# A split float32 two-block model on one core: squares added ahead of the feed-forward, h passed on tile by tile, a weight half moved among squares, and the copy of y moved

## The chip, the cores and the metric

The kernel runs as one program on one core of a Trainium2 chip. The metric is the device time of one execution in microseconds (us), lower is better. A core has TensorE (PE, matmuls into eight PSUM banks), VectorE (DVE), ScalarE (ACT), GpSimd (POOL) and SyncE (SP, which here issues nearly all DMAs). Each engine runs its own list of instructions in order; they meet only at semaphores, and an instruction that waits holds back everything behind it on its engine.

## The reference

One batch of 256 tokens, width 1024, float32. Two blocks follow one another, each with two layers.

```
first_block, per layer: proj = x @ w_in -> three attention branches
   (8 MoBA heads, 8 MLA heads, 4 differential heads), each gated and merged,
   out projection, layer norm, a gated per-layer embedding
second_block, per layer i:
   h = rmsnorm(x, norm_mix[i]);  x = x + hybrid_mixer(h)     # gated conv, SSD, conformer conv
   h = rmsnorm(x, norm_ffn[i])
   i = 0: x = x + (silu(h @ w_gate) * (h @ w_up)) @ w_down   # dense, 2816 wide
   i = 1: x = x + mixture of 8 experts, 2 per token, 3584 wide
y = rmsnorm(x, norm_final)
rmsnorm(x, g) = x * rsqrt(mean(x*x) + eps) * g
```

## The kernel before, in words

**Layout.** The activation x lies in SBUF as `xT`: eight tiles (`DT = 8`) of 128 features by 256 tokens. A projection takes a weight unit of 1024 x 256 (1 MB), lands it in one of three slots of a ring, and multiplies it with all eight tiles.

**Split products.** float32 products are made of three passes in a faster format. Each operand is cut into a high part (a rounded copy) and a low part (the value less the high part). ACT makes the high part of a weight unit in two halves of 128x1024 (`split`, semaphore `hi_done`), POOL or DVE makes the low part of each half (`lo_done`), and PE adds up high x high, low-weight x high and high-weight x low. For 256 columns that is 48 matmuls a unit. A ring slot is free for SP's next DMA when the low parts of both halves are made (`slot_freed`). The high and low weight buffers have two slots each, so ACT may split unit q + 2 as soon as PE has used unit q. `after("mc0")` in `layer_body` is such a call: it waits for a landing, then splits the unit two places behind `mc0`, which is `az0`.

**First block.** The order of PE's work is the list `ORDER1`. Around `mc0` it is: `dv0`, `dv1`, the first half of `mc0`, step B1 (transposes of the probabilities of attention batch 1 into banks 4 to 6), step M (the second half of `mc0`), V1 (`pv`: probabilities times values into bank 7), A2 (`scores` of batch 2: twelve matmuls that need banks 4, 5 and 6 back, then four that need bank 7 back), then `mc1`, `mc2`. ACT copies the turned probabilities out (`take_turned(1)`, 3 copies, semaphore `pT_ready`, which V1 waits for), and copies bank 7 out (`take_y(1)`, semaphore `y_ready`, which the last four matmuls of A2 wait for). ACT's written order is: drain of `dv1`, `take_turned(1)`, both halves of `after("mc0")`, `take_y(1)`, `latent(0)`. Both layers of the first block run it.

**The three norms that the change touches.** (1) Ahead of mixer 0, (2) ahead of the feed-forward (`norm(1)`), (3) ahead of mixer 1. In each, ACT squares pairs of tiles of x, PE multiplies the eight tiles of squares with a matrix of 1/1024 to get the mean on all partitions, ACT takes Ln and Exp (`inv_std`), DVE makes h, eight instructions of one tile (L2362), ACT copies the high part of h in four pairs (`high_parts`, semaphore `hh_ready`), DVE makes the low part in four pairs after all of h (`low_part`, `hl_ready`). PE then starts on the first weight unit with `split_project_first`: high x high of tiles 0 to 3 for both column halves, low weights of the first column half for these tiles, the same for tiles 4 to 7, low weights of the second column half, and at the end high weights x low h. Between the mean and the first unit PE runs some matmuls on zeros (`keep_busy`).

**Around them.** In `norm(1)` PE runs the last output projections `wo0` to `wo3`; DVE adds each to x, ACT squares it. ACT makes the first half of the `gate` unit before Ln and Exp and the second half behind them; DVE makes the low part of the first half before h and of the second behind it. Ahead of mixer 1, x is updated by four additions on DVE (`add_sums`, semaphore `x_up`), ACT squares each pair, loads the table for Ln and Exp, waits for the mean, and after Exp makes the second high half of the unit `gv`, whose low half POOL makes.

Of the kernel before, what the change touches and what calls it, by code (L numbers as in the profile page):

```python
# [35 lines left out]
P = 128  # L36
# [223 lines left out]
def build_kernel(nc, a, out):  # L260

    ctx = ExitStack()
    with ctx:
# [172 lines left out]
        h_part, hh_ready, hl_ready = (signal(n, 4) for n in ("h_tiles_ready", "h_high_ready", "h_low_ready"))  # L436
# [34 lines left out]
        dt_neg, dt_w = signal("dt_neg_abs", 1), signal("dt_exp_plus_1", 1)  # L471
# [11 lines left out]
        centred = signal("ln_centred", 4)  # L483
        vlink = signal("vector_step")
# [229 lines left out]
        def _(pe):  # L714
# [19 lines left out]
            def split_project(b, slot, lo_at, x, count, settled=False):  # L734

                wh, wl = (w[:, slot, :].rearrange("p (k n) -> p k n", n=S) for w in (whi, wlo))
                for t in range(2):
# [9 lines left out]
                    ins.then_inc((used if t == 0 else count).h, 1)  # L747

# [384 lines left out]
            def wait_h(k):  # L1133

                return (lambda pair: pe.wait_ge(hh_ready.h, hh_ready.at(k, pair + 1)),
                        lambda pair: pe.wait_ge(hl_ready.h, hl_ready.at(k, pair + 1)))
# [22 lines left out]
            def mixer(m):  # L1159
# [39 lines left out]
                for name, _ in ORDER2:  # L1199
# [103 lines left out]
                    elif name == "gg":  # L1303
                        split_project_first(begin(name), *take_split(full2), *wait_h(2 * m))
                    else:
                        split_project(begin(name), *take_split(full2))

            def norm(n):
# [4 lines left out]
                for kk in range(DT):  # L1313
                    if kk % 2 == 0:
                        pe.wait_ge(nrm["sq"].h, 4 * (n - 1) + kk // 2 + 1)
                    ins = mm(views(0)[:, 0, :], ONES[D], sq[:, kk, :], kk == 0, kk == DT - 1)
# [39 lines left out]
            split_project_first(0, *take_split(ff_full), *wait_h(1))  # L1356
# [311 lines left out]
        def _(act):  # L1668
# [67 lines left out]
            def layer_body(layer):  # L1736
# [86 lines left out]
                drain(layer, "dv1", dv[:, :, S:512])  # L1823
                take_turned(1)

# [5 lines left out]
                after("mc0")  # L1831
                take_y(1)
# [176 lines left out]
            def high_parts(k):  # L2009

                for n in range(4):
                    act.wait_ge(h_part.h, h_part.at(k, n + 1))
                    copy(hh[:, 2 * n:2 * n + 2, :], h[:, 2 * n:2 * n + 2, :]).then_inc(hh_ready.h, 1)

            def mixer(m):
# [43 lines left out]
                act.wait_ge(dt_neg.h, dt_neg.at(m, 1))  # L2059
# [4 lines left out]
                act.wait_ge(dt_w.h, dt_w.at(m, 1))  # L2064
# [285 lines left out]
        def _(dve):  # L2350
# [214 lines left out]
            def low_part(k, n):  # L2565

                dve.wait_ge(hh_ready.h, hh_ready.at(k, n + 1))
# [16 lines left out]
            def mixer(m):  # L2584
# [15 lines left out]
                for t in range(DT):  # L2600
                    ins = stt(h[:, t, :], xT[:, t, :], q2[:, Q_NM + t:Q_NM + t + 1], rs2[:, 0, :],
                              ALU.mult, ALU.mult)
                    if t % 2:
                        ins.then_inc(h_part.h, 1)
# [585 lines left out]
```

## Time and profile before

| what | value |
|---|---|
| time, median of 3 runs | 2121.65 us (2121.0 to 2123.34) |
| the profiled execution: its own time | 2121.3 us |
| the profiled execution: span from first to last instruction | 2119.5 us |
| mean granted TensorE clock | 0.997 |
| busy: PE, DVE, ACT, POOL | 2096.3, 1416.4, 1295.4, 651.4 us |
| DMA, over the span | 529.06 MB, mean 250 GB/s |

The span is shorter than the execution's own time by 1.8 us, which lies outside the instructions. Times in rows are microseconds from the start of the span. `[0.84 <-ACT y L1673]` behind a row of a timeline means that the engine was idle for 0.84 us before it, until ACT's write to y released it. L720 is the one line where matmuls are issued, L1670 and L1673 those of ACT's functions and copies; their tiles tell them apart. A timeline merges like instructions in a row (x8), with the time from the first start to the last end.

### The profile page before, as it was taken

To read this page: it belongs to the slowest core of one execution; us is meant where nothing else is said; L and a number is where in the kernel's file an instruction comes from. 1 tells how busy PE (TensorE), PEld (TensorE's weight loads), DVE (VectorE), ACT (ScalarE), POOL (GpSimd) and SP (SyncE) were. 2 spreads that over 40 slices of the span, in tenths; PEclk is the share of its full clock that TensorE was granted. 3 is DMA by queue.
4 is the path that set the end of the run, shared out by engine and by line. 5 is a ranking of instruction groups with operands and counts; after the bars stand their busy time and mean duration, and the time that the engine had idled before them with its cause. 6 is when DMAs were issued, how large, how long until landed. Compare 5 with 4: busy or idle time off the path is not lost.

```text
span 2119.5 us, 33547 instructions
## 1 busy us (share of the span) xinstructions
PE 2096.3 (99%) x13311; PEld 1867.1 (88%) x13315; DVE 1416.4 (67%) x1437; ACT 1295.4 (61%) x1424; POOL 651.4 (31%) x316
## 2 busy tenths in 40 slices
PE   9999999999999999999999999999999999999998
PEld 8979999988999999999998888888888888888887
DVE  1555223346422774223777999999999999999997
ACT  4556545455544534444545777777777777777776
POOL 5717886726787204988101000000000000000000
PEclk9999999999999999999999999999999999999999
DMA  7434564625455425655447999999999999999995
GB/s 245 138 105 153 179 198 156 183 75 163 160 188 177 129 91 175 189 193 178 141 140 252 387 376 336 370 360 376 352 351 370 351 375 351 359 356 375 367 365 200
DMA packets 307633, 529.06 MB, mean 250 GB/s; under 512 B 11842, under 2 KB 152802, under 8 KB 307520
## 3 DMA queue, kind: packets, MB, share of 16 engines
q1 hardware_dynamic: 306496, 525.92, 70.9%
q8 instruction: 84, 1.38, 0.3%
q0 software_dynamic: 736, 1.00, 0.2%
q10 hardware_dynamic: 288, 0.52, 0.1%
q14 instruction: 29, 0.24, 0.0%
HBM read 525.84 MB, written 1.05 MB: 249 GB/s over the span
## 4 chain that ended last, share of the span: by engine, by line
PE 90%; POOL 3%; DVE 3%; ACT 2%; DMA 1%; issue 1%; SPq 0%; DVEq 0%; POOLq 0%
PE bank L720 88%; POOL weights_low L3092 3%; PE bank L1525 1%; DVE qb L2354 1%; DMA ring<-in_w_in_dram 1%; ACT sc L1670 1%; ACT weights_high L1673 0%; DVE sc L2362 0%; DMA ring<-in_w_ple_dram 0%; DVE h L2362 0%; PE bank L929 0%; PE bank L731 0%; DVE nmax L2389 0%; ACT expert_weights_high L1673 0%; ACT xT L1670 0%
## 5 line engine op out<-in xcount | busy, mean ns | idle before, releaser
L2354 DVE TENSOR_TENSOR expert_weights_low<-ring_experts,expert_weights_high 128x2048 fp32r<-128x2048 f32 x336 | 764.7, 2288 | 72.6 <-ACT expert_weights_high L1673 72.5
L1673 ACT ACTIVATE expert_weights_high<-ring_experts 128x2048 fp32r<-128x2048 f32 x336 | 646.4, 1924 | 166.3 <-PE bank L720 162.2
L3092 POOL TENSOR_TENSOR weights_low<-ring,weights_high 128x1024 fp32r<-128x1024 f32 x252 | 617.5, 2474 | 332.0 <-ACT weights_high L1673 218.8
L1673 ACT ACTIVATE weights_high<-ring 128x1024 fp32r<-128x1024 f32 x294 | 303.9, 1056 | 331.7 <-PE bank L720 293.0
L720 PE MATMUL bank<-x_high,weights_high 128*128 128x256 f32 x1024 | 229.8, 281 | 0.5 <-POOL weights_low L3092 0.4
L720 PE MATMUL bank<-x_high,weights_low 128*128 128x256 f32 x1024 | 226.2, 277 | 0.0
L720 PEld LDWEIGHTS bank<-x_high,weights_high 128*128 128x128 f32 x1024 | 183.6, 188 | 2.5 <-POOL weights_low L3092 0.8
L720 PEld LDWEIGHTS bank<-x_high,weights_low 128*128 128x128 f32 x1024 | 183.3, 188 | 0.5 <-issue 0.5
L720 PE MATMUL bank<-expert_weights_high,gathered_high 128*128 128x512 f32 x456 | 180.7, 396 | 0.4 <-DVE gathered_low L2362 0.4
L720 PE MATMUL bank<-expert_weights_high,gathered_low 128*128 128x512 f32 x456 | 177.8, 390 | 0.0
L720 PE MATMUL bank<-expert_weights_high,gathered_high_b 128*128 128x512 f32 x448 | 177.6, 396 | 0.0
L720 PE MATMUL bank<-expert_weights_high,gathered_low_b 128*128 128x512 f32 x448 | 174.7, 390 | 0.0
L720 PE MATMUL bank<-expert_weights_high,hidden_turned_low 128*128 128x512 f32 x440 | 171.3, 389 | 0.0
L720 PE MATMUL bank<-expert_weights_high,hidden_turned_high 128*128 128x512 f32 x440 | 171.2, 389 | 0.0
L720 PE MATMUL bank<-h_high,weights_high 128*128 128x256 f32 x704 | 164.0, 283 | 5.1 <-ACT h_high L1673 5.1
L720 PE MATMUL bank<-h_high,weights_low 128*128 128x256 f32 x704 | 161.6, 281 | 0.0
L720 PEld LDWEIGHTS bank<-h_high,weights_high 128*128 128x128 f32 x704 | 131.1, 192 | 7.7 <-ACT weights_high L1673 2.9
L720 PE MATMUL bank<-x_low,weights_high 128*128 128x256 f32 x1024 | 137.4, 277 | 0.0
L720 PEld LDWEIGHTS bank<-h_high,weights_low 128*128 128x128 f32 x704 | 130.6, 192 | 0.0
L720 PEld LDWEIGHTS bank<-x_low,weights_high 128*128 128x128 f32 x1024 | 126.3, 188 | 0.0
L720 PE MATMUL bank<-expert_weights_low,gathered_high 128*128 128x512 f32 x456 | 122.3, 390 | 0.0
L720 PE MATMUL bank<-expert_weights_low,gathered_high_b 128*128 128x512 f32 x448 | 120.0, 390 | 0.0
(338 smaller groups left out, 3724.7 us busy)
## 6 DMA issues: line engine op xcount, KB each, us to landing
ring_experts<-in_moe_w_gate_dram SPq DMA_DIRECT2D x112, 1024.0 KB, 6.0
ring_experts<-in_moe_w_up_dram SPq DMA_DIRECT2D x112, 1024.0 KB, 5.8
ring_experts<-in_moe_w_down_dram SPq DMA_DIRECT2D x112, 1024.0 KB, 5.4
ring<-in_w_in_dram SPq DMA_DIRECT2D x62, 1024.0 KB, 5.3
ring<-in_w_merge_dram SPq DMA_DIRECT2D x24, 1024.0 KB, 5.1
ring<-in_w_out_dram SPq DMA_DIRECT2D x14, 1024.0 KB, 5.1
ring<-in_ffn_w_gate_dram SPq DMA_DIRECT2D x11, 1024.0 KB, 5.4
ring<-in_ffn_w_up_dram SPq DMA_DIRECT2D x11, 1024.0 KB, 5.3
```

The lines of the kernel that those rows point to most:

```text
L720: ins = pe.matmul(dst, w, x, start=start, stop=stop, skip_group_check=share)
L1525: ins = pe.transpose(bank[2][:, c * P:(c + 1) * P], hd[:, c * P:(c + 1) * P], ident)
L1670: return nc.scalar.activation(dst, src, func, **kw)
L1673: return nc.scalar.activation(dst, src, ACT.Copy, scale=scale)
L2354: return nc.vector.tensor_tensor(dst, x, z, op)
L3092: nc.gpsimd.tensor_tensor(half_of(wlo[:, q_slot, :], t, width), half_of(ring[:, slot, :], t, width), half_of(whi[:, q_slot, :], t, width). ...
```

## The change

Five edits.

1. **h tile by tile.** DVE signals each tile of h, ACT copies it alone (8 copies of 128x256 for 4 of 128x512), and PE starts with a new function `split_project_h`: for each tile, high x high and low weights of the first column half, then high x high of the second, and low weights of the second too in the mixers (`staged=False`); in the feed-forward (`staged=True`) these last come when their low half is made. It waits at its start for the low weights that it needs.
2. **Two pairs of squares are added.** In mixer 0, after the third addition to x, DVE adds the squares of tiles 0 and 1 to those of tiles 2 and 3. `norm(1)` sums six tiles instead of eight.
3. **Mixer 1, ACT's order.** The table load goes ahead of the four squares, and the second high half of `gv` goes between the second and the third square.
4. **First block, ACT's order.** `after("mc0")` is taken apart: its first half goes ahead of `take_turned(1)`, then `take_turned(1)`, `take_y(1)`, and then its second half.
5. Two semaphores, `dt_neg` and `dt_w`, become one counted to two. No instruction is added by it.

```diff
+            def split_project_h(b, slot, lo_at, x, count, wait_high, wait_low, staged):
+                pe.wait_ge(hi_done.h, lo_at + 1)
+                pe.wait_ge(lo_done.h, lo_at + (0 if staged else 1))
+                for kk in range(DT):
+                    wait_high(kk)
+                    for t in range(2):
+                        mm(views(b)[:, t, :], wh[:, kk, t * P:(t + 1) * P], x[0][:, kk, :],
+                           kk == 0 and t == 0, False, share=True)
+                        if t == 0 or not staged:
+                            mm(views(b)[:, t, :], wl[:, kk, t * P:(t + 1) * P], x[0][:, kk, :], False, False, share=True)
+                if staged:
+                    pe.wait_ge(lo_done.h, lo_at + 1)
+                    for kk in range(DT):
+                        mm(views(b)[:, 1, :], wl[:, kk, P:2 * P], x[0][:, kk, :], False, False, share=True)
+                for kk in range(DT):
+                    if kk % 2 == 0:
+                        wait_low(kk // 2)
+                    for t in range(2):
+                        ins = mm(views(b)[:, t, :], wh[:, kk, t * P:(t + 1) * P], x[1][:, kk, :], False, ...)
...
# mixers' "gg" and the first gate unit of the feed-forward
-                        split_project_first(begin(name), *take_split(full2), *wait_h(2 * m))
+                        split_project_h(begin(name), *take_split(full2), *wait_h(2 * m), staged=False)
-            split_project_first(0, *take_split(ff_full), *wait_h(1))
+            split_project_h(0, *take_split(ff_full), *wait_h(1), staged=True)
...
# norm(n) on PE
+                first = 2 if n == 1 else 0
+                if n == 1:
+                    pe.wait_ge(sq_added.h, 1)
-                for kk in range(DT):
+                for kk in range(first, DT):
...
# first block, ACT
                 drain(layer, "dv1", dv[:, :, S:512])
+                after("mc0", (0,))
                 take_turned(1)
+                take_y(1)
+                after("mc0", (1,))
...
-                after("mc0")
-                take_y(1)
                 latent(0)
...
# high_parts, ACT
-                for n in range(4):
-                    act.wait_ge(h_part.h, h_part.at(k, n + 1))
-                    copy(hh[:, 2 * n:2 * n + 2, :], h[:, 2 * n:2 * n + 2, :]).then_inc(hh_ready.h, 1)
+                for t in range(DT):
+                    act.wait_ge(h_part.h, h_part.at(k, t + 1))
+                    copy(hh[:, t, :], h[:, t, :]).then_inc(hh_ready.h, 1)
...
# mixer 1, ACT
                 if m:
+                    act.preload_act_table_set(LOG_EXP)
                     for j in range(4):
                         act.wait_ge(x_up.h, j + 1)
                         square(j).then_inc(sq_ready.h, 1)
-                    act.preload_act_table_set(LOG_EXP)
+                        if j == 1:
+                            split2(SPLITS_M + 1, lambda t: act.wait_ge(ff_down.h, 4 * FD), halves=(1,))
                 b = G2.wait_full(act, m, "ms")
                 inv_std(rs2[:, 0, :], views(b)[:, 0, :], 0, d2a.h, drained2_at("ms")).then_inc(std_ready.h, 1)
-                if m:
-                    split2(SPLITS_M + 1, lambda t: act.wait_ge(ff_down.h, 4 * FD), halves=(1,))
                 high_parts(2 * m)
...
# mixer, DVE, after each addition of wo{j} to xT
+                    if m == 0 and j == 2:
+                        dve.wait_ge(nrm["sq"].h, 2)
+                        tt_(sq[:, 2:4, :], sq[:, 2:4, :], sq[:, 0:2, :], ALU.add).then_inc(sq_added.h, 1)
...
# low_part, DVE
-                dve.wait_ge(hh_ready.h, hh_ready.at(k, n + 1))
+                dve.wait_ge(hh_ready.h, hh_ready.at(k, 2 * n + 2))
```

## Rows read from the trace of the kernel before

**Rows 1.** The page, part 1: busy time and share of the span by engine.

```profile
PE 2096.3 (99%) x13311; PEld 1867.1 (88%) x13315; DVE 1416.4 (67%) x1437; ACT 1295.4 (61%) x1424; POOL 651.4 (31%) x316
```

**Rows 2.** The chain of waits, first block, layer 0: start, us, what.

```profile
93.75 5.21 DMA ring<-in_w_in_dram
98.99 2.00 ACT weights_high L1673 x2
101.00 0.49 ACT y L1673
...
101.53 13.60 PE bank L720 x84
```

**Rows 3.** ACT's timeline, the same stretch: start, us, instruction, [idle before].

```profile
94.99 1.58 ACT L1673 ACTIVATE pT<-bank 128x512 f32<-128x512 f32 x3 [1.50 <-PE bank L929]
```

**Rows 4.** PE's timeline, the same stretch.

```profile
97.62 1.57 PE L720 MATMUL bank<-pT,av 128*64 128x256 f32 x16
99.12 1.57 PE L720 MATMUL bank<-dqk 64*128 64x256 f32 x12
101.53 0.71 PE L720 MATMUL bank<-dqk 64*128 64x128 f32 x4 [0.84 <-ACT y L1673]
```

**Rows 5.** ACT's timeline, first block, layer 1.

```profile
436.74 2.00 ACT L1673 ACTIVATE weights_high<-ring 128x1024 fp32r<-128x1024 f32 x2 [2.51 <-DMA ring<-in_w_in_dram]
```

**Rows 6.** ACT's timeline ahead of mixer 0.

```profile
687.81 3.31 ACT L1670 ACTIVATE sq<-qb,par 128x256 f32<-128x256 f32 x8 [0.55 <-DVE qb L2362]
...
694.45 0.63 ACT L1673 ACTIVATE h_high<-h 128x512 fp32r<-128x512 f32 x1 [1.00 <-DVE h L2362]
```

**Rows 7.** DVE's timeline ahead of mixer 0.

```profile
693.54 3.26 DVE L2362 SCALAR_TENSOR_TENSOR h<-xT,q,rs 128x256 f32<-128x256 f32 x8 [1.05 <-issue]
696.72 2.49 DVE L2354 TENSOR_TENSOR h_low<-h,h_high 128x512 fp32r<-128x512 f32 x4
```

**Rows 8.** PE's timeline at the start of mixer 0.

```profile
695.23 1.44 PE L720 MATMUL bank<-h_high,weights_high 128*128 128x256 f32 x8 [1.01 <-ACT h_high L1673]
...
699.45 1.98 PE L720 MATMUL bank<-h_low,weights_high 128*128 128x256 f32 x16
701.26 0.28 PE L720 MATMUL bank<-h_high,weights_high 128*128 128x256 f32 x1
```

**Rows 9.** PE's timeline ahead of the feed-forward and in its first unit.

```profile
810.43 3.62 PE L720 MATMUL bank<-sq,ones 128*128 128x256 f32 x16
...
822.76 1.07 PE L720 MATMUL bank<-h_high,weights_high 128*128 128x256 f32 x8
```

**Rows 10.** DVE's timeline ahead of the feed-forward.

```profile
813.03 1.23 DVE L2354 TENSOR_TENSOR weights_low<-ring,weights_high 128x1024 fp32r<-128x1024 f32 x1 [1.71 <-ACT weights_high L1673]
815.04 3.26 DVE L2362 SCALAR_TENSOR_TENSOR h<-xT,q,rs 128x256 f32<-128x256 f32 x8 [0.78 <-ACT rs L1670]
```

**Rows 11.** ACT's timeline ahead of the feed-forward.

```profile
814.91 1.04 ACT L1673 ACTIVATE weights_high<-ring 128x1024 fp32r<-128x1024 f32 x1
```

**Rows 12.** ACT's timeline ahead of mixer 1.

```profile
995.31 1.06 ACT L1673 ACTIVATE weights_high<-ring 128x1024 fp32r<-128x1024 f32 x1 [1.66 <-PE bank L720]
...
999.40 1.28 ACT L2024 ACT_TABLE_LOAD   x1
```

**Rows 13.** DVE's timeline ahead of mixer 1.

```profile
1002.52 5.35 DVE L2362 SCALAR_TENSOR_TENSOR h<-xT,q,rs 128x256 f32<-128x256 f32 x8 [3.41 <-ACT rs L1670]
```

**Rows 14.** POOL's timeline, the same stretch.

```profile
1003.43 2.57 POOL L3092 TENSOR_TENSOR weights_low<-ring,weights_high 128x1024 fp32r<-128x1024 f32 x1 [4.58 <-ACT weights_high L1673]
```

**Rows 15.** PE's timeline ahead of mixer 1 and in its first unit.

```profile
997.83 3.61 PE L720 MATMUL bank<-sq,ones 128*128 128x256 f32 x16
...
1007.00 0.84 PE L720 MATMUL bank<-h_high,weights_high 128*128 128x256 f32 x4 [2.09 <-ACT h_high L1673]
...
1013.74 0.28 PE L720 MATMUL bank<-h_high,weights_high 128*128 128x256 f32 x1
```

**Rows 16.** Busy time by stretch: start:end, us, PE, PEld, DVE, ACT, POOL, clock, DMA share, GB/s.

```profile
1007.00:1011.00 4.00, 4.00 (x21) 4.00 (x22) 3.28 (x7) 1.26 (x2) 0.54 (x1) 0.57 0.16 12
```

More of the change, by code:

```diff
@@ L435, in build_kernel @@
         wo3_in, router_in = signal("last_out_weights_landed", 16), sem("router_weights_landed")
-        h_part, hh_ready, hl_ready = (signal(n, 4) for n in ("h_tiles_ready", "h_high_ready", "h_low_ready"))
+        h_part, hh_ready, hl_ready = (signal(n, k) for n, k in (
+            ("h_tiles_ready", DT), ("h_high_ready", DT), ("h_low_ready", 4)))
         first_units = N_UNITS1 * LAYERS
@@ L483, in build_kernel @@
         centred = signal("ln_centred", 4)
+        sq_added = signal("first_pairs_of_squares_added")
         vlink = signal("vector_step")
@@ L747, in split_project @@
                     ins.then_inc((used if t == 0 else count).h, 1)
+            def split_project_h(b, slot, lo_at, x, count, wait_high, wait_low, staged):
+                wh, wl = (w[:, slot, :].rearrange("p (k n) -> p k n", n=S) for w in (whi, wlo))
+                pe.wait_ge(hi_done.h, lo_at + 1)
[15 more added lines that the diff above has]
+                    for t in range(2):
+                        ins = mm(views(b)[:, t, :], wh[:, kk, t * P:(t + 1) * P], x[1][:, kk, :], False,
+                                 kk == DT - 1, share=True)
+                        if kk == DT - 1:
+                            ins.then_inc((used if t == 0 else count).h, 1)
             def split_project_low_last(b, slot, lo_at, x, count, halves=(0, 1)):
@@ L1312, in norm @@
                     G2.wait_drained(pe, n - 1, [g for g in G2.names if G2.index(g) % BANKS2 == 0][-1])
-                for kk in range(DT):
+                first = 2 if n == 1 else 0
+                if n == 1:
+                    pe.wait_ge(sq_added.h, 1)
+                for kk in range(first, DT):
                     if kk % 2 == 0:
                         pe.wait_ge(nrm["sq"].h, 4 * (n - 1) + kk // 2 + 1)
-                    ins = mm(views(0)[:, 0, :], ONES[D], sq[:, kk, :], kk == 0, kk == DT - 1)
+                    ins = mm(views(0)[:, 0, :], ONES[D], sq[:, kk, :], kk == first, kk == DT - 1)
                 ins.then_inc(nrm["full"].h, 1)
@@ L2063, in mixer @@
                 pad(2)
-                act.wait_ge(dt_w.h, dt_w.at(m, 1))
+                act.wait_ge(dt_step.h, dt_step.at(m, 2))
                 fn(dtt[:, 4, :], dtt[:, 3, :], ACT.Ln).then_inc(dtl.h, 1)
@@ L2715, in mixer @@
                 conv_x(2)
-                dve.wait_ge(dt_w.h, dt_w.at(m, 1))
+                dve.wait_ge(dt_step.h, dt_step.at(m, 2))
                 step_sizes()
@@ L2799, in norm @@
                     ins = stt(dst[:, t, :], xT[:, t, :], q2[:, w + t:w + t + 1], rs2[:, 0, :], ALU.mult, ALU.mult)
-                    if n == 1 and t % 2:
+                    if n == 1:
                         ins.then_inc(h_part.h, 1)
```

15 lines of the change are left out of this document (7 added, 8 removed).

## The prediction

> **What bounds the kernel now.** I read the busy times by engine first: PE is busy for 99% of the span [rows 1], and the chain of waits is nearly all PE. So a gain or a loss counts only where PE stands still, or where it is set back by something ahead of it. Then I read the chain and the timelines at the places that the diff touches.
>
> In the first block the chain at `mc0` is DMA, ACT, PE: the weights of `az0` land at 98.96 us, ACT splits both halves (2.00 us), copies y, and PE goes on at 101.53 us [rows 2]. ACT had copied the turned probabilities before that, at 94.99 us [rows 3], so that PE could run V1 at 97.62 us, right behind the second half of `mc0`, and stood idle only 0.84 us ahead of the last four matmuls of A2 [rows 4]. Layer 1 has the same wait of ACT for the landing [rows 5]. At the three norms PE waits for std, h and h's high parts [rows 8, 9 and 15].
>
> **Edit 4, ACT's order at mc0.** The reader should see that the half now put ahead of `take_turned(1)` can't start before its weights land, and that nothing in the change makes them land sooner: the transfer is issued at 93.75 us and takes 5.21 us, behind POOL's low parts [rows 2]. So ACT, which took up the probabilities at 94.99 us, now stands at the wait until 98.99 us. Queued behind it are the probabilities, y and the second half, and PE waits for the first of them. One half takes 1.00 us (two took 2.00), so `take_turned(1)` runs from 99.99 to 101.57 us (1.58 us) [rows 3], and V1 starts near 101.6 us instead of 97.62 us: PE is idle for 4.0 us in one piece. V1 and the first twelve matmuls of A2 take 3.07 us (97.62 us to where the idle 0.84 us began, 100.69 us) [rows 4]. y is copied during those twelve matmuls, so the old wait of 0.84 us goes. The last four matmuls start near 101.6 + 3.07 = 104.65 us instead of 101.53 us: 3.1 us later. PE is the chain for the 13.60 us behind this point [rows 2], and the softmax of batch 2 starts from those same scores, so I see no cover that takes it back. The second half of `az0` is done near 104.7 us, long before its use behind `mc2`, `uq` and the rest. Two layers: **+6.2 us**.
>
> **The clock in these stalls.** Ahead of mixer 1 PE stood still for most of 1003 to 1007 us (one idle piece of 2.09 us at its end) [rows 15], and behind it the granted clock was 0.57 over 4 us [rows 16], which is a time mostly at the lower level, 1.2 GHz. That costs (1 - 0.57) x 4 = 1.7 us of PE's work. A stall of 4.0 us in one piece is longer than that one. Bounds for each layer: 0, if the clock stays up, and 2 x 1.7 = 3.4 us, if two such stretches follow. I take 1.4 us, near the row, and less than it because part of the slow stretch can fall into the idle time itself. Two layers: **+2.8 us**.
>
> The Trainium skill, "TensorE: Matmul & The Clock Gate", section "Why this matters for your kernels", says that idle gaps between bursts of matmuls bring the engine back to its half rate. By that rule both stalls are followed by a slow stretch, which is what the row ahead of mixer 1 shows; without it the sum below would be 2.8 us less.
>
> **Edit 1 ahead of mixer 0.** DVE makes the eight tiles in 3.26 us, 0.40 us apart (the last takes 0.48) [rows 7]. ACT's first copy started 0.91 us behind DVE's start, after two tiles, and PE 0.78 us behind that [rows 6 and 8]. With one tile: the tile is there at 0.50 us, ACT's copy of 256 columns takes 0.49 us (eight squares of that size took 3.31 us, so they follow each other 0.40 us apart, even with a wait each) [rows 6], and PE needs 0.15 us more: start near 693.54 + 1.16 = 694.7 us instead of 695.23 us. PE then has four matmuls a tile. Sixteen take 1.81 us (699.45 to 701.26 us) [rows 8], so four take 0.45 us, longer than ACT's 0.40 us: PE is not starved. 32 matmuls end at 694.7 + 3.63 = 698.3 us, and the sixteen with low h at 700.15 us. The low parts come 0.62 us apart from 696.72 us on, the last at 699.2 us [rows 7], before PE wants it (699.7 us). The old end is 701.26 us: **-1.1 us**. Where ACT's copies keep 0.56 us instead, the gain is 0.2 us. The next unit starts from PE's end through ACT and DVE, so it moves along.
>
> **Edits 1 and 2 ahead of the feed-forward.** The sum over eight tiles takes 3.62 us, 0.45 us a tile, from 810.43 us [rows 9]; six end at 813.15 us, 0.9 us sooner. The added instruction has the size of one of `low_part` (128x512, four in 2.49 us, so some 0.65 us) [rows 7] and fits between DVE's third addition and the fourth (which wait 1.04 us for PE): it hides there, at nothing; if it were late, PE would lose what it lacks, up to 0.7 us. Std is ready near 814.2 us, but DVE is busy with the low half from 813.03 to 814.26 us, so h starts there instead of at 815.04 us [rows 10]: -0.76 us. ACT's second gate half (1.04 us) [rows 11] now starts at 814.0 us, and the first tile of h waits for it until 815.0 us; PE starts near 815.6 us, is paced by ACT to 818.75 us (three matmuls a tile, 0.34 us against 0.40 us), does the eight of the second column half until 819.7 us, and is then paced by the low parts, which come 0.76 us sooner than before, the last at 821.1 us. End near 821.6 us against 822.76 us [rows 9]: **-1.2 us**.
>
> **Edits 1 and 3 ahead of mixer 1.** DVE's eight tiles took 5.35 us here [rows 13] against 3.26 us [rows 7], and the difference lies in one of them, which ran beside POOL's low half at 1003.43 us for 2.57 us [rows 14]. With ACT's high half of `gv` among the squares, POOL's part runs near 999.9 to 1002.4 us, before h: -2.1 us. The price: the table load (1.28 us) follows ACT's last split (995.31 + 1.06 us) [rows 12], so the first square starts at 997.65 us and PE's sum at 998.3 us instead of 997.83 us; the split pushes the third square to 999.7 us, for which PE waits 0.2 us more. The sum ends near 1002.2 us instead of 1001.44 us: +0.7 us. h starts at 1003.25 us, PE at 1004.4 us, its first unit ends at 1009.85 us as in mixer 0 (5.44 us), against 1013.74 us [rows 15]: **-3.9 us**. In this lies the slow clock behind the old stall, which I take to be gone.
>
> The Trainium skill, "GPSIMD Engine Reference", section "Key points", says that GpSimd contends with VectorE instructions that have two SBUF inputs. h is made by such instructions, and the long one agrees; by that rule h is free of it in the new order, since POOL has nothing else to do then.
>
> **Edit 5** adds no instruction: 0. **SP and the DMAs**: no transfer is added; those of `az0` keep their time, the others move with PE.
>
> **Sum.** +6.2 + 2.8 - 1.1 - 1.2 - 3.9 = **+2.8 us** on the profiled execution: 2119.5 + 2.8 = 2122.3 us of span, and 2124.1 us with the 1.8 us around it. That execution lay 0.35 us below the median, 2121.65 us; on the median it is 2124.4 us. It is +0.13%, and I call a difference within 0.2% (4.2 us) no change, which is about what a measurement of this kernel can tell.
>
> **The rivals.**
> - *The copies of h are slower than I take them* (slower). If ACT needs 0.56 us for a tile, its waits not hidden, PE is starved at each norm: 7 x 0.11 = 0.8 us less gained in each of the three places. Net +5.2 us: 2126.9 us. It decides above 0.47 us a copy (1.4 us over the three). For it: pairs of h came with a gap of 0.16 us each. Against: the eight squares at 0.40 us apart.
> - *The half clock outlasts one stretch* (slower). Two in each layer: 6.8 us instead of 2.8, net +6.8 us: 2128.4 us. It decides from 2.1 us a layer. Against: ahead of mixer 1 one stretch was all.
> - *The stall is there, the clock stays up* (no change): 2121.6 us. Against: rows 16.
> - *The probabilities aren't held up* (faster), because the landing comes before 95 us. Then PE keeps V1, the idle 0.84 us (and as much in layer 1) goes too: -6.2 - 1.8 = -8.0 us: 2113.7 us. For it: only the order as written. Against: the landing sits in the chain, 2.5 us after ACT was free even behind `take_turned(1)` in layer 1 [rows 5]. This is also the case where the change does what it says, y sooner.
>
> **How the numbers follow.** Forecast 0.52 (its own range 2121.5 to 2127.5), slow copies 0.14, long half clock 0.13, clock stays up 0.14, no hold-up 0.07. Slower by over 0.2% (above 2125.9 us) takes both slow rivals and 0.09 of the forecast: 0.36. Faster (below 2117.4 us) is the last rival: 0.07. The rest, 0.57, is within 0.2%. The range 2118.5 to 2129.0 us leaves out the last rival and the far end of the slow ones.
>
> **What would show it.** ACT idle 2.4 us or more on a DMA ahead of one `weights_high`, then the copies to pT at 100 us (layer 1: near 441 us); PE idle about 4 us ahead of its matmuls with pT in both layers, and no wait for y; a clock below 1.0 in the 4 us behind. At the norms: h in 3.3 us ahead of mixer 1 and no long tile, eight copies to h_high 0.40 us apart, first units ending 5.4 us after their start. I am wrong if pT is copied at 95 us, if copies are 0.5 us apart or more, or if PE has new waits for DVE or ACT inside the mixers.

## The result

The changed kernel takes 2124.58 us (median of 20 runs, 2121.03 to 2127.43) against 2121.17 us of the kernel before (median of 20 runs, 2118.45 to 2124.62). The ratio is 1.0017, with a 95% interval of 1.0011 to 1.0023: slower by 3.4 us. The loss is small but clear of the noise, since the whole interval lies above 1. The profiled execution took 2123.14 us with a span of 2121.3 us and a mean granted clock of 0.996, and lies 1.4 us below the median of the changed kernel.

The timelines give how much later the changed kernel is at each place that both kernels have. The shift less the one before it is what the stretch between them cost.

| place | before | changed | shift |
|---|---|---|---|
| DMA of `az0` issued, layer 0 | 93.75 | 94.33 | +0.58 |
| first unit behind A2, layer 0 | 102.17 | 105.20 | +3.03 |
| DMA of `az0` issued, layer 1 | 431.41 | 433.91 | +2.50 |
| first unit behind A2, layer 1 | 439.92 | 446.34 | +6.42 |
| first tile of h, mixer 0 | 693.54 | 699.43 | +5.89 |
| second unit of mixer 0 | 701.26 | 706.05 | +4.79 |
| sum of squares ahead of the feed-forward | 810.43 | 816.04 | +5.61 |
| second unit of the feed-forward | 822.76 | 827.22 | +4.46 |
| first addition to x ahead of mixer 1 | 995.99 | 1000.44 | +4.45 |
| second unit of mixer 1 | 1013.74 | 1014.68 | +0.94 |
| end | 2119.5 | 2121.3 | +1.8 |

### The profile page after: what moved, and what is told of

It reads as the page before. It is cut to its first block, busy times and chain, and to the rows that moved or that the text cites. A ratio compares the mean times of both kernels' runs of the same rounds, so it can differ in the third digit from the quotient of the medians.

```text
span 2121.3 us, 33554 instructions
## 1 busy us (share of the span) xinstructions
PE 2094.5 (99%) x13307; PEld 1864.9 (88%) x13311; DVE 1413.6 (67%) x1438; ACT 1296.4 (61%) x1436; POOL 654.5 (31%) x316
## 4 chain that ended last, share of the span: by engine, by line
PE 90%; POOL 3%; DVE 3%; ACT 2%; DMA 1%; issue 1%; SPq 0%; DVEq 0%; POOLq 0%; ACTq 0%
PE bank L722 88%; POOL weights_low L3125 3%; PE bank L1555 1%; DVE qb L2385 1%; DMA ring<-in_w_in_dram 1%; ACT sc L1700 1%; DVE sc L2393 0%; DMA ring<-in_w_ple_dram 0%; ACT weights_high L1703 0%; PE bank L956 0%; PE bank L733 0%; DVE nmax L2420 0%; ACT xT L1700 0%; DVE y L2393 0%; ACT sq L1700 0%
## 5 line engine op out<-in xcount | busy, mean ns | idle before, releaser
L722 PE MATMUL bank<-h_high,weights_low 128*128 128x256 f32 x704 | 166.3, 281 | 0.0
```

Source lines behind the costliest of these rows:

```text
L722: ins = pe.matmul(dst, w, x, start=start, stop=stop, skip_group_check=share)
```

## The profile after

**At mc0.** ACT's timeline in layer 0, which answers to [rows 2 and 3].

```profile
99.52 1.06 ACT L1703 ACTIVATE weights_high<-ring 128x1024 fp32r<-128x1024 f32 x1 [5.45 <-DMA ring<-in_w_in_dram]
100.48 1.55 ACT L1703 ACTIVATE pT<-bank 128x512 f32<-128x512 f32 x3
103.69 0.60 ACT L1703 ACTIVATE y<-bank 128x512 f32<-128x512 f32 x1 [1.66 <-PE bank L722]
104.19 1.05 ACT L1703 ACTIVATE weights_high<-ring 128x1024 fp32r<-128x1024 f32 x1
```

ACT is idle for 5.45 us until the landing; the probabilities, which it took at 94.99 us [rows 3], come 5.5 us later. PE's timeline in both layers, which answers to [rows 4]:

```profile
102.08 1.57 PE L722 MATMUL bank<-pT,av 128*64 128x256 f32 x16 [3.82 <-ACT pT L1703]
103.59 1.68 PE L722 MATMUL bank<-dqk 64*128 64x256 f32 x16
...
441.79 2.88 PE L722 MATMUL bank<-pT,av 128*64 128x256 f32 x16 [3.95 <-ACT pT L1703]
444.61 1.80 PE L722 MATMUL bank<-dqk 64*128 64x256 f32 x16
```

PE is idle for 3.82 and 3.95 us in one piece. All sixteen matmuls of A2 are one row now: the wait for y is gone. In layer 0 V1 takes 1.57 us as before, in layer 1 it takes 2.88 us. Busy time by stretch tells why; the third number from the right is the granted clock.

```profile
98.00:102.00 4.00, 0.27 (x3) 0.07 (x1) 0.00 (x0) 2.48 (x4) 2.32 (x2) 1.00 0.50 153
441.00:445.00 4.00, 3.21 (x18) 2.24 (x20) 0.00 (x0) 1.03 (x3) 1.70 (x1) 0.57 0.01 3
```

The granted clock fell to the lower level, 1.2 GHz, at the stall of layer 1 (0.57 over these 4 us) and not at that of layer 0 (1.00). It fell at 441.5 us, 0.3 us before V1 starts.

**Ahead of mixer 0.** ACT's eight copies, and PE's low part of the first unit [rows 6 and 8]:

```profile
699.95 3.19 ACT L1703 ACTIVATE h_high<-h 128x256 fp32r<-128x256 f32 x8 [0.61 <-DVE h L2393]
```

```profile
704.24 1.98 PE L722 MATMUL bank<-h_low,weights_high 128*128 128x256 f32 x16
```

Eight copies in 3.19 us are 0.39 us apart, which is the pace of DVE's tiles (0.40 us apart). Ahead of the feed-forward, where ACT starts late and the tiles are ready, eight take 2.89 us (820.61 us on), 0.35 us apart. From the first tile of h to the low part is 4.81 us (699.43 to 704.24 us) against 5.91 us before.

**Ahead of the feed-forward.** DVE's timeline, then PE's, which answer to [rows 9 and 10]:

```profile
815.12 0.68 DVE L2385 TENSOR_TENSOR sq<-sq 128x512 f32<-128x512 f32 x1
816.25 0.69 DVE L2385 TENSOR_TENSOR xT<-xT,bank 128x512 f32<-128x512 f32 x1 [0.44 <-PE bank L722]
818.65 1.23 DVE L2385 TENSOR_TENSOR weights_low<-ring,weights_high 128x1024 fp32r<-128x1024 f32 x1 [1.71 <-ACT weights_high L1703]
819.79 3.25 DVE L2393 SCALAR_TENSOR_TENSOR h<-xT,q,rs 128x256 f32<-128x256 f32 x8
```

```profile
816.04 2.75 PE L722 MATMUL bank<-sq,ones 128*128 128x256 f32 x12
```

The added instruction takes 0.68 us in DVE's idle time, of which 0.44 us is left. PE doesn't wait for it, and its sum is 2.75 us instead of 3.62 us. h begins as soon as DVE's low half lets it: no idle time stands before it.

**Ahead of mixer 1.** DVE, POOL and PE, which answer to [rows 13 to 15]:

```profile
1007.87 3.26 DVE L2393 SCALAR_TENSOR_TENSOR h<-xT,q,rs 128x256 f32<-128x256 f32 x8 [4.31 <-ACT rs L1700]
```

```profile
1004.31 2.35 POOL L3125 TENSOR_TENSOR weights_low<-ring,weights_high 128x1024 fp32r<-128x1024 f32 x1 [1.02 <-ACT weights_high L1703]
```

```profile
1002.82 3.98 PE L722 MATMUL bank<-sq,ones 128*128 128x256 f32 x16 [0.38 <-ACT sq L1700]
```

POOL is done at 1006.66 us, before h. h has no long tile: 3.26 us against 5.35 us. The sum of squares starts behind 0.38 us of idle time and takes 3.98 us against 3.61 us. It also starts later, 2.38 us behind the first addition to x (1000.44 us) against 1.84 us before (995.99 us). Together that is 0.9 us, the price of the table load ahead of the squares and of the split among them.

## The experiments

All times are medians; the kernel before, run on the same chip beside each series, took 2120.79 us in the first series (e1 to e4) and 2120.50 us in the second (f1 to f4).

### e1: the order at mc0 alone

The kernel before, with:

```diff
+                after("mc0", (0,))
                 take_turned(1)
+                take_y(1)
+                after("mc0", (1,))
...
-                after("mc0")
-                take_y(1)
```

> The kernel before with edit 4 alone (first half of az0 ahead of take_turned(1), take_y(1), then the second half). My theory: PE stands still for some 3.9 us ahead of V1 in both layers, loses about 2.5 us a layer by it (the first unit behind A2 starts 3.03 us later in layer 0 of the changed kernel, of which 0.58 us was there before the stall), and about 1.5 us more in each layer where the granted clock falls behind the stall: +5 to +8 us, most likely +7.9 us, 2129 us. Rival A (the order costs nothing, the loss of the whole change lies elsewhere): within 1 us of before. Rival B (the stall costs its 2.5 us a layer but the clock costs nothing in time): +5 us, 2126 us.

Measured: 2128.73 us (2126.87 to 2131.88), ratio 1.0038 (1.0026 to 1.0050), +7.9 us. PE's timeline in both layers, and the busy time by stretch:

```profile
100.92 1.82 PE L720 MATMUL bank<-pT,av 128*64 128x256 f32 x16 [4.03 <-ACT pT L1673]
102.67 3.03 PE L720 MATMUL bank<-dqk 64*128 64x256 f32 x16
...
442.43 2.00 PE L720 MATMUL bank<-pT,av 128*64 128x256 f32 x16 [3.97 <-ACT pT L1673]
444.36 2.86 PE L720 MATMUL bank<-dqk 64*128 64x256 f32 x16
```

```profile
101.00:105.00 4.00, 4.00 (x29) 3.13 (x31) 0.00 (x0) 2.22 (x4) 1.43 (x2) 0.64 0.00 0
442.00:446.00 4.00, 3.57 (x24) 2.74 (x25) 0.00 (x0) 1.91 (x4) 1.35 (x1) 0.68 0.00 0
```

Here the clock fell in both layers, and V1 with A2 took 4.7 us in each where 3.12 us do at the full clock. The slow clock cost 1.6 us in each. Rival A is out, by the median and by the stalls. The interval (5.5 to 10.6 us) leaves out rival B's 5 us, narrowly; e4 tests that point by itself.

### e2: the changed kernel with that order undone

> The changed kernel with edit 4 undone. My theory: only the gains at the three norms are left, which the anchors of the two traces give as -1.1 (mixer 0), -1.15 (feed-forward) and -3.5 us (mixer 1): -5.7 us against before, 2115.4 us. Rival A (the norms gain little, and the order at mc0 costs little): 2119 to 2121 us. If the terms add up, this run's difference and e1's add up to the difference of the whole change, +3.4 us.

Its edit is that of e1 the other way round. Measured: 2115.05 us (2113.75 to 2116.6), ratio 0.9973 (0.9962 to 0.9984), -5.7 us. The norms gain what the shifts in the first table give for the three places (1.10, 1.15 and 3.51 us, together 5.8 us). The differences of e1 and e2 add up to +2.2 us against +3.4 us for the whole change, which is within what the intervals leave.

### e3: y sooner, without the wait

The changed kernel, with:

```diff
-                after("mc0", (0,))
                 take_turned(1)
                 take_y(1)
-                after("mc0", (1,))
+                after("mc0")
```

> The changed kernel with ACT's order at mc0 as take_turned(1), take_y(1), then both halves of az0: the copy of y sooner without a wait for the landing ahead of the probabilities. My theory: V1 starts behind the second half of mc0 as before, y is copied during the first twelve matmuls of A2, and the idle time ahead of the last four goes: from V1's start to the next unit's start 3.1 us instead of 4.55 us, so -1.4 us a layer against e2: about 2112.6 us. Rival: the halves of az0 come some 0.7 us later, and with them latent(0), POOL's low parts and the next transfers, and PE waits for one of them: the gain against e2 is under 1 us over both layers, 2114.5 us or more.

Measured: 2113.17 us (2110.34 to 2114.49), ratio 0.9963 (0.9951 to 0.9976). PE's timeline in layer 0, and ACT's:

```profile
97.98 1.57 PE L722 MATMUL bank<-pT,av 128*64 128x256 f32 x16
99.48 1.68 PE L722 MATMUL bank<-dqk 64*128 64x256 f32 x16
```

```profile
99.59 0.60 ACT L1703 ACTIVATE y<-bank 128x512 f32<-128x512 f32 x1 [2.66 <-PE bank L722]
100.08 2.00 ACT L1703 ACTIVATE weights_high<-ring 128x1024 fp32r<-128x1024 f32 x2
```

No idle time of PE is left at this place. In e2, which has the old order here, PE still waits for y:

```profile
102.32 0.71 PE L722 MATMUL bank<-dqk 64*128 64x128 f32 x4 [0.78 <-ACT y L1703]
```

From V1's start to the next unit is 3.12 us (97.98 to 101.10 us) against 4.49 us in e2 (98.47 to 102.96 us): 1.4 us a layer, as expected. The split starts 0.7 us behind the landing (the transfer was issued at 94.12 us and took 5.3 us). The medians of e2 and e3 differ by 1.9 us, less than 2 x 1.4, but their intervals overlap, so the medians alone settle neither the theory nor the rival's 1 us; the trace shows the mechanism.

### e4: PE kept busy in the stall

The changed kernel, with:

```diff
                     elif name == "V":
+                        if who == 1:
+                            keep_busy(7, 14)
                         pv(who)
```

> The changed kernel with 14 matmuls on zeros into bank 7 ahead of PE's wait for pT in V1 of batch 1, in both layers (some 3 us of the 3.9 us of idle time; V1 overwrites bank 7). The stall stays. My theory (part of the loss is the clock behind the stall): the clock stays at 1.00 there, PE's 28 matmuls behind it take 3.1 us in both layers, and the time is 1.5 to 3 us below the changed kernel, some 2122 us. Rival (the clock behind the stall costs nothing in time, or falls all the same): 2124.6 us as the changed kernel.

Measured: 2121.80 us (2117.72 to 2122.84), ratio 1.0000 (0.9991 to 1.0009). PE's timeline in layer 1 and the busy time by stretch of both layers:

```profile
437.62 3.20 PE L854 MATMUL bank<-zeros 128*128 128x512 bf16 x14
441.78 1.57 PE L722 MATMUL bank<-pT,av 128*64 128x256 f32 x16 [0.96 <-ACT pT L1705]
```

```profile
102.00:106.00 4.00, 3.73 (x37) 3.17 (x38) 0.51 (x2) 2.34 (x5) 1.68 (x2) 1.00 0.00 0
442.00:446.00 4.00, 4.00 (x41) 3.45 (x38) 1.00 (x4) 2.52 (x4) 1.68 (x2) 1.00 0.02 4
```

V1 still starts when the probabilities are there (441.78 us, 441.79 us in the changed kernel), but it takes 1.57 us instead of 2.88 us. The medians of e4 and of the changed kernel differ by 2.8 us and the ratios by 0.0017, which is 3.6 us. The two were not run in one series, and by their intervals the difference is somewhere between 1 and 6 us (an estimate), so the rival that the slow clock costs nothing is out. About 3 us of the loss was the slow clock at the stalls; what is left of the loss at `mc0` is the idle time itself. The two profiled executions differ by only 0.3 us in their times, though e4 gains 1.4 us in layer 1. Against that stands the spacing of matmuls, told below: e4's trace has 1966 neighbouring matmuls at the wider of two spacings, the changed kernel's 1523, some 2 us more (an estimate).

### f1: h tile by tile alone

The kernel before with `split_project_h` in place of `split_project_first`, a signal and a copy for each tile, and the shared signal of `dt` (edit 5):

```diff
-                for n in range(4):
-                    act.wait_ge(h_part.h, h_part.at(k, n + 1))
-                    copy(hh[:, 2 * n:2 * n + 2, :], h[:, 2 * n:2 * n + 2, :]).then_inc(hh_ready.h, 1)
+                for t in range(DT):
+                    act.wait_ge(h_part.h, h_part.at(k, t + 1))
+                    copy(hh[:, t, :], h[:, t, :]).then_inc(hh_ready.h, 1)
...
-                    if t % 2:
-                        ins.then_inc(h_part.h, 1)
+                    ins.then_inc(h_part.h, 1)
```

> The kernel before with edit 1 alone (h signalled, copied and multiplied tile by tile in all three norms). My theory: mixer 0 gains 1.1 us and the feed-forward some 0.5 us (std is as late as before). Ahead of mixer 1 POOL's low half still runs beside h, so one tile of h still takes over 2 us and h still takes 5.3 us; PE starts at the first tile and stands still at the fourth: 2 to 2.8 us gained there. Together -3.5 to -4.4 us, 2117 us. Rival (the last tile of h sets the end, so finer steps give nothing where one is long): mixer 1 gains under 1 us, 2119 us.

Measured: 2116.55 us (2113.95 to 2119.19), ratio 0.9980 (0.9971 to 0.9989), -4.0 us. DVE, POOL and ACT ahead of mixer 1:

```profile
1002.08 5.39 DVE L2388 SCALAR_TENSOR_TENSOR h<-xT,q,rs 128x256 f32<-128x256 f32 x8 [3.41 <-ACT rs L1696]
```

```profile
1002.99 2.61 POOL L3117 TENSOR_TENSOR weights_low<-ring,weights_high 128x1024 fp32r<-128x1024 f32 x1 [4.59 <-ACT weights_high L1699]
```

```profile
1002.82 1.01 ACT L1699 ACTIVATE h_high<-h 128x256 fp32r<-128x256 f32 x3
1005.92 2.00 ACT L1699 ACTIVATE h_high<-h 128x256 fp32r<-128x256 f32 x5 [2.08 <-DVE h L2388]
```

The long tile is there again. But PE worked through three tiles before it, so the idle time was 0.63 us and then 1.41 us in place of 1.03 us and 2.09 us, and the clock did not fall in the first unit:

```profile
1003.37 0.36 PE L721 MATMUL bank<-h_high,weights_high 128*128 128x256 f32 x1 [0.63 <-ACT h_high L1699]
...
1006.39 0.39 PE L721 MATMUL bank<-h_high,weights_high 128*128 128x256 f32 x1 [1.41 <-ACT h_high L1699]
```

```profile
1006.00:1010.00 4.00, 3.61 (x31) 3.61 (x32) 3.88 (x8) 1.92 (x5) 0.00 (x0) 1.00 0.16 12
```

This answers to [rows 16], 0.57 there. The rival is out: from the first addition to x to the second unit is 15.04 us (995.55 to 1010.59 us) against 17.75 us before.

### f2: the added squares alone

> The kernel before with edits 2 and 5 alone (DVE adds two pairs of squares, PE sums six tiles; the two dt semaphores are one). My theory: PE's sum ends 0.9 us sooner, but DVE is busy with the low half of the gate unit, so h starts 0.76 us sooner and the end moves by 0.75 us: 2120.1 us, hardly to be told from before. The added instruction lies in DVE's idle time and PE doesn't wait for it. Rival (it is late and PE waits): no gain, 2120.8 us, with an idle time of PE ahead of its sum.

The kernel before has no semaphore left for the added signal, so the two signals of `dt` are one here, as in the changed kernel: edit 5 is what makes room for edit 2. The loop of PE's sum and DVE's addition are:

```diff
-                for kk in range(DT):
+                first = 2 if n == 1 else 0
+                if n == 1:
+                    pe.wait_ge(sq_added.h, 1)
+                for kk in range(first, DT):
...
+                    if m == 0 and j == 2:
+                        dve.wait_ge(nrm["sq"].h, 2)
+                        tt_(sq[:, 2:4, :], sq[:, 2:4, :], sq[:, 0:2, :], ALU.add).then_inc(sq_added.h, 1)
```

Measured: 2120.44 us (2117.75 to 2122.5), ratio 0.9997 (0.9988 to 1.0006): inconclusive by time, since what was at stake is less than the interval. DVE's timeline tells more:

```profile
810.54 0.68 DVE L2358 TENSOR_TENSOR sq<-sq 128x512 f32<-128x512 f32 x1
811.67 0.69 DVE L2358 TENSOR_TENSOR xT<-xT,bank 128x512 f32<-128x512 f32 x1 [0.44 <-PE bank L721]
814.07 1.23 DVE L2358 TENSOR_TENSOR weights_low<-ring,weights_high 128x1024 fp32r<-128x1024 f32 x1 [1.71 <-ACT weights_high L1677]
815.21 3.25 DVE L2366 SCALAR_TENSOR_TENSOR h<-xT,q,rs 128x256 f32<-128x256 f32 x8
```

The added instruction has 0.44 us of idle time behind it, so the fourth addition to x isn't late. h starts 3.54 us behind that addition (811.67 to 815.21 us) against 4.41 us before (810.63 to 815.04 us), and the second unit 11.39 us behind it (823.06 us) against 12.13 us: 0.74 us gained on PE, where the prediction had 0.76 us.

### f3: the order ahead of mixer 1 alone

The kernel before, with the table load ahead of the squares and the half of `gv` among them:

```diff
                 if m:
+                    act.preload_act_table_set(LOG_EXP)
                     for j in range(4):
                         act.wait_ge(x_up.h, j + 1)
                         square(j).then_inc(sq_ready.h, 1)
-                    act.preload_act_table_set(LOG_EXP)
+                        if j == 1:
+                            split2(SPLITS_M + 1, lambda t: act.wait_ge(ff_down.h, 4 * FD), halves=(1,))
                 b = G2.wait_full(act, m, "ms")
                 inv_std(rs2[:, 0, :], views(b)[:, 0, :], 0, d2a.h, drained2_at("ms")).then_inc(std_ready.h, 1)
-                if m:
-                    split2(SPLITS_M + 1, lambda t: act.wait_ge(ff_down.h, 4 * FD), halves=(1,))
```

> The kernel before with edit 3 alone (table load ahead of the squares, the high half of gv between the second and third). My theory: POOL's low half runs before h, so h takes 3.3 us instead of 5.3 us with no long tile, it starts 0.7 to 0.9 us later, and the clock no longer falls in the first unit of mixer 1: -2.4 to -2.8 us, 2118.3 us. Rival A (h's long tile has nothing to do with POOL): h keeps its long tile and the time is 0.8 us above before. Rival B (the clock fell for another cause): it falls again, and only about 1.3 us are gained.

Measured: 2117.58 us (2115.29 to 2119.26), ratio 0.9984 (0.9975 to 0.9993), -2.9 us. DVE, POOL and PE:

```profile
1003.14 3.26 DVE L2362 SCALAR_TENSOR_TENSOR h<-xT,q,rs 128x256 f32<-128x256 f32 x8 [4.31 <-ACT rs L1670]
```

```profile
999.58 2.35 POOL L3092 TENSOR_TENSOR weights_low<-ring,weights_high 128x1024 fp32r<-128x1024 f32 x1 [1.03 <-ACT weights_high L1673]
```

```profile
998.08 3.98 PE L720 MATMUL bank<-sq,ones 128*128 128x256 f32 x16 [0.38 <-ACT sq L1670]
...
1004.82 1.44 PE L720 MATMUL bank<-h_high,weights_high 128*128 128x256 f32 x8 [1.03 <-ACT h_high L1673]
```

POOL ends at 1001.93 us, 1.2 us before h, and h has no long tile. The reader should compare the last row with [rows 15]: the idle 2.09 us in the middle of the first unit is gone, and only the 1.03 us ahead of it, as at mixer 0 [rows 8], is left. The clock there is 1.00:

```profile
1004.00:1008.00 4.00, 3.18 (x23) 2.87 (x24) 4.00 (x10) 2.53 (x4) 0.00 (x0) 1.00 0.00 0
```

From the first addition to x to the second unit is 15.16 us (995.70 to 1010.86 us) against 17.75 us before: 2.6 us, and the median has 2.9 us. So the order alone mends the long tile and with it the slow clock. f1 mends the clock in another way, with the long tile still there (15.04 us), and both together give 14.24 us (1000.44 to 1014.68 us in the changed kernel): 2.7 and 2.6 us by themselves, 3.5 us and not 5.3 us together. Each takes away the same fall of the clock, which cost 1.4 to 1.6 us where it could be read by itself (at `mc0`). That is most of the missing 1.8 us; how the rest divides no run shows.

### f4: y ahead, and the table behind the squares

The kernel of e3, with:

```diff
                 if m:
-                    act.preload_act_table_set(LOG_EXP)
                     for j in range(4):
                         act.wait_ge(x_up.h, j + 1)
                         square(j).then_inc(sq_ready.h, 1)
                         if j == 1:
                             split2(SPLITS_M + 1, lambda t: act.wait_ge(ff_down.h, 4 * FD), halves=(1,))
+                    act.preload_act_table_set(LOG_EXP)
```

> The kernel of e3 with the table load put back behind the four squares of mixer 1, the high half of gv still between the second and the third. My theory: the first square starts when x is there, some 1 us sooner, the table is loaded while PE sums, and h starts as early as in the kernel before or 0.1 us behind it: 0.7 to 0.9 us less than e3, 2112.3 us. Rival (the split between the squares sets the sum's end, or the table load then comes too late): as e3, 2113.2 us. From the medians alone this can't be told; the start of h against the last addition to x in the trace tells it.

Measured: 2110.94 us (2109.43 to 2111.56), ratio 0.9951 (0.9938 to 0.9965): 9.6 us below the kernel before in the same series and the fastest of all; the median of the changed kernel, from another series, is 13.6 us higher. ACT's timeline, and DVE's:

```profile
991.71 1.31 ACT L1700 ACTIVATE sq<-xT 128x512 f32<-128x512 f32 x2 [0.34 <-DVE xT L2384]
993.09 1.06 ACT L1703 ACTIVATE weights_high<-ring 128x1024 fp32r<-128x1024 f32 x1
994.05 1.14 ACT L1700 ACTIVATE sq<-xT 128x512 f32<-128x512 f32 x2
995.20 1.28 ACT L2056 ACT_TABLE_LOAD   x1
996.75 0.47 ACT L1700 ACTIVATE rs<-bank,eps 128x256 f32<-128x256 f32 x1 [0.27 <-PE bank L722]
```

```profile
997.78 3.26 DVE L2392 SCALAR_TENSOR_TENSOR h<-xT,q,rs 128x256 f32<-128x256 f32 x8 [3.67 <-ACT rs L1700]
```

The load ends at 996.48 us, 0.27 us before the sum is there: it costs nothing behind the squares. h starts 6.79 us behind the first addition to x (990.99 us), against 7.44 us in e3 (989.40 to 996.84 us), and the second unit 13.42 us behind it (1004.41 us) against 14.06 us in e3 (1003.46 us). The row of h in e3:

```profile
996.84 3.26 DVE L2392 SCALAR_TENSOR_TENSOR h<-xT,q,rs 128x256 f32<-128x256 f32 x8 [4.31 <-ACT rs L1700]
```

So the place of the load is worth 0.65 us, a little less than the 0.7 to 0.9 us expected. (The changed kernel has 14.24 us in place of e3's 14.06 us, but its matmuls were further apart in that unit, as told in the next section.) The medians of e3 and f4 are 2.2 us apart, more than that, but they are from two series and their intervals overlap: only the trace carries this point.

## Why the prediction was right

The forecast was 2124.4 us and no measurable change, by five terms of both signs. The time came out at 2124.58 us, +0.17%, within the 0.2% that it called no change. As a difference, +2.8 us was forecast and +3.4 us was measured: the kernel before had a median of 2121.65 us in the three runs that the forecast started from and of 2121.17 us in the twenty beside the changed kernel. The forecast held 0.2% to be about what a measurement can tell; twenty runs of each told 0.06%. Its terms, one by one:

- **The stall at `mc0`, +6.2 us: right in kind, too large.** The half waits for the landing, the probabilities behind it, and PE for them: V1 starts 3.9 us later in layer 0, once the 0.58 us by which the transfer was issued later are taken off (102.08 - 0.58 - 97.62). But the loss at the next unit is 2.45 us (3.03 - 0.58), not 3.1 us. The step that was off is "V1 and the first twelve matmuls of A2 take 3.07 us": that went to the end of the twelfth, and then let the last four cost what they had. All 32 matmuls take 3.12 us to the next unit when nothing stops them (102.08 to 105.20 us), where they took 4.55 us before (97.62 to 102.17 us), 0.84 us of it idle and 0.64 us for four matmuls behind a halt (101.53 to 102.17 us). So the halt that went was worth 1.4 us, and not 0.9 us. Two layers: 4.9 us. e3 shows the same 1.4 us without any stall.
- **The clock behind the stalls, +2.8 us: right, as far as can be told.** e4 puts it at about 3 us, with a wide interval. In one layer it is 1.4 us when it comes (4.55 us against 3.12 us from V1 to the next unit), and 1.6 us in e1. The rows give no more than that it came in layer 1 of the changed kernel and in both of e1, and not in layer 0 of the changed kernel. So the profiled execution shows half of it. It lies 1.4 us below the median, as much as one such fall costs, but of the other runs only the mean granted clock of the whole is on record, and where it fell there no trace shows. These means fit a fall in both layers in most of them: the six runs of e1 were granted 0.9952 in the mean against 0.9968 for the kernel before beside them, and 0.0016 of 2120 us is 3.4 us (an estimate), where two falls of 1.6 us make 3.2 us. The twenty of the changed kernel were granted 0.9953 and the eleven of e4 0.9975. The Trainium skill, "TensorE: Matmul & The Clock Gate", section "Why this matters for your kernels", has idle gaps bring the engine back to its half rate. The traces agree in three of four such gaps, of 3.95 to 4.03 us, and disagree in the one of 3.82 us.
- **Mixer 0, -1.1 us: right.** -1.10 us (the shift goes from 5.89 to 4.79 us). ACT's copies are 0.39 us apart, so the rival of slow copies is out.
- **The feed-forward, -1.2 us: right.** -1.15 us (5.61 to 4.46 us); f2 shows 0.74 us of it alone.
- **Mixer 1, -3.9 us: nearly right.** -3.51 us (4.45 to 0.94 us). Two steps fell short. The price was put at "+0.7 us" for the later sum. h starts 7.43 us behind the first addition to x (1000.44 to 1007.87 us) against 6.53 us before (995.99 to 1002.52 us), +0.9 us. The larger part is in the first unit: it took 5.73 us (1008.95 to 1014.68 us), where 5.44 us was forecast and mixer 0 took 5.54 us (700.51 to 706.05 us). Its matmuls were 0.118 us apart from its start to its end, those of mixer 0 mostly 0.113 us; over 48 matmuls that makes 0.2 us. In e3, with 0.113 us, the same unit took 5.55 us (997.91 to 1003.46 us). What sets the one spacing or the other no run shows; the granted clock was 1.00 with both.
- **Edit 5, 0: right.** It adds no instruction; it is there to free a semaphore for edit 2. No run has it alone, but f2, which has it beside edit 2, shows no loss.

The profiled execution can be added up. Its terms are 4.9 us of stall, 1.5 us of clock (one layer), -1.10, -1.15 and -3.51 us, together +0.6 us. The rest of its +1.8 us lies between the places that the edits touch: +0.58 us ahead of `mc0`, -0.53 us between the layers, -0.53 us ahead of mixer 0, +0.82 us inside mixer 0, -0.01 us in the feed-forward and +0.86 us behind the second unit of mixer 1, +1.2 us in all. The forecast had nothing for that. The two traces show where most of it comes from, and it is in no wait that the edits made. Neighbouring 128x256 matmuls follow each other either 0.113 or 0.118 us apart, and how many do which differs. Counted from the first unit behind A2 in layer 0 to the issue of `az0` in layer 1, 682 were at the wider spacing before and 529 in the changed kernel, and from the first unit behind A2 in layer 1 to mixer 0 it was 286 against 147. At 0.0045 us apiece that makes some 0.7 and 0.6 us less (estimates), where -0.53 us was read for each. Behind the second unit of mixer 1 it was 395 against 562, some 0.8 us more (an estimate), where +0.86 us was read. Inside mixer 0 it was 275 against 99, some 0.8 us less (an estimate), but there the clock was also low for longer:

```profile
700.00:745.00 45.00, 45.00 (x379) 45.00 (x378) 36.03 (x70) 24.86 (x31) 11.30 (x14) 0.96 0.53 164
700.00:745.00 45.00, 44.60 (x365) 44.52 (x365) 35.56 (x71) 24.86 (x35) 12.45 (x14) 0.92 0.45 141
```

The first row is the kernel before, the second the changed one: 0.04 of 45 us is 1.8 us more. Together that is +1.0 us, where +0.82 us was read. The +0.58 us ahead of `mc0` stays unexplained.

So, if the median holds the full term for the clock, three errors stand behind a difference that is 0.6 us off: the stall 1.3 us too dear, mixer 1 0.4 us too good, the rest, 1.2 us in the profiled execution, left out. They partly cancel, and that the time itself is only 0.2 us off is partly luck, in the lower median of the kernel before too; the signs, the places and the order of the sizes are not.

Of the rivals, slow copies are out by the 0.39 us (and 0.35 us ahead of the feed-forward), and the probabilities that aren't held up by ACT's 5.45 us of idle time. The half clock that outlasts one stretch is out: one stretch is all in the rows, and the term is 1.4 to 1.6 us a layer in them. The bound that the prediction gave for slow copies, 0.47 us, doesn't follow from its own numbers: with PE's 0.45 us a tile, 1.4 us over three places and seven tiles each makes it 0.52 us. Nothing hangs on it, since the copies lie below both. "The stall is there, the clock stays up" is true of layer 0 in the profiled execution; for the kernel as a whole it is what e4 builds, about 3 us faster than the changed kernel.

## What to carry to other kernels

When an instruction is moved ahead in an engine's order, look first at what it waits for: a wait on a transfer holds up everything queued behind it, and here one weight half with 5 us to wait cost PE 2.5 us a layer and some 1.5 us more where the clock fell, while y, the point of the edit, was worth 1.4 us a layer as soon as it went ahead without the wait (e3, f4). When a halt of PE in the middle of a run goes, count from the start of the run to the start of the next unit, not to the end of the last matmul before it. And gains that remove the same fall of the clock don't add up (f1 and f3).

## What the runs showed of the hardware

- DVE and POOL. One tile of h takes 2.6 us instead of 0.48 us beside POOL's low half (before, f1 and f2), and none does where POOL is done before (the changed kernel, f3, f4). It is one tile of the eight: in f1 the tiles take 0.473 us at least, 0.476 us in the median and 2.611 us at most, and POOL's instruction takes 2.61 us. The Trainium skill, "GPSIMD Engine Reference", section "Key points", names contention with VectorE instructions that are in a 2-port perf mode or have two SBUF inputs; the traces agree for h, which has two. In the kernel before a CAST with one input also took 2.40 us, at 829.20 us beside POOL, where the changed kernel has 0.43 us (833.65 us). So two inputs are not needed for it; whether the CAST ran in such a mode no trace shows.
- The clock also falls without idle time of PE. In mixer 1 of every kernel, and in mixer 0 of every one but e1 and f3, it falls at the 32 matmuls with 8 columns of `dt`, which take 3.9 us in the kernel before: while they run, or at most 1.4 us behind the start of the last. Over 700 to 745 us, with PE busy for 45.00 us of 45.00, the kernel before was granted 0.96, f3 1.00 and f2 0.92, with nearly the same PE work; the changed kernel was granted 0.92 with PE busy for 44.60 us. So it varies from one execution to the next.
- The spread of each kernel's times goes with the granted clock. Of the 27 runs of the kernel before beside f1 to f4, the ten with a mean granted clock of 0.998 took 2117.36 to 2120.72 us and the two with 0.995 took 2122.85 to 2123.12 us; 0.003 of 2120 us is 6.4 us (an estimate), and the fastest and the slowest of the twenty runs beside the changed kernel are 6.2 us apart. Runs of one granted clock still differ by 3 us, so the clock is not the whole of it; the spacing below may be a part, which no run tested.
- The spacing of dense 128x256 matmuls takes one of two values, 0.113 and 0.118 us, at a granted clock of 1.00. The same stretch of the same work has now more of one and now more of the other (529 of the wider ones between the layers in the changed kernel, 682 in the kernel before), and no run shows why.
